# Second MLP matmul as seven block products, in a two-layer decoder trunk on eight cores

## The chip, the cores and the metric

One Trainium2 chip, all 8 cores. Each core runs the same program on its own two of the 16 sequences (4096 tokens); the cores do not exchange data. The metric is the device time of one execution in microseconds, that of the slowest core. TensorE does the matmuls, VectorE, ScalarE and GpSimd the elementwise work, and each of these engines works through its own queue strictly in order.

## The reference

Two layers on h of shape (16, 2048, 1024), D_MODEL 1024, D_FF 4096, and a final norm:

```python
def squared_relu_mlp(h, w1, w2):
    a = jax.nn.relu(h @ w1)
    return (a * a) @ w2

for i in range(DEPTH):               # DEPTH = 2
    if i == 0: h = h + conv_mixers(rms_norm(h, ...), ...)
    else:      h = h + chunked_spatial_gating(rms_norm(h, ...), ...)
    h = h + squared_relu_mlp(rms_norm(h, mlp_norm_g[i]), mlp_w1[i], mlp_w2[i])
return rms_norm(h, final_norm_g)
```

Only the MLP is changed. Its two matmuls are 1024 x 4096 and 4096 x 1024 for each token.

## The kernel before

A core makes four passes (`mt`) over 1024 tokens each. In a pass: mixer 0, MLP 0, mixer 1, MLP 1. `h` (float32) and the transposed normed activations `xnT` (float16) stay in SBUF for the pass. There are 8 PSUM banks, handed out from a list in order of release (`get_bank`, `put_bank`).

**Weights** are cut into pieces, which go through 7 slots of 8 KB per partition in a fixed order; `release(i)` frees a slot and at once asks for the next pieces. On its first use a piece is *fresh*: it is read as float32 and cast by the DMA, which GpSimd's queue issues; the prepared piece is then written to a cache in DRAM (`wcache`). Later passes load it from there, issued by the SP queue. Which pass is the first use for the cache is `first_mt`: for `w1_1` passes 0 and 1 both load fresh and pass 1 stores.

**The MLP** (`mlp`) runs in four quarters `fq` of the hidden width, each first matmul, then second.

First matmul: four pieces a quarter. `Job` computes 128 x 2 hidden columns for all 1024 tokens as a 2 x 2 block product with seven products instead of eight (Winograd's form). One product is 4 matmuls of 128 x 128 on 128 x 512. The operands on the activation side are four blocks of `xnT` and four sums of them (`Xs`, made by `xsum`); on the weight side four blocks and four differences, made on VectorE by `prep` for fresh pieces (for a cached piece they come with it). The methods are A (products m1, m2), B7 (m7), B6 (m6), C (m5), D4 (m4), D3 (m3). m6, m5 and m3 accumulate into the bank of m1, and m4 into that of m7; between them ScalarE takes a copy (`snap`) and VectorE adds the bank to such a copy (`via`). So each of these products must wait until the reader before it has read the bank. Then comes `relu_sq`: relu on ScalarE, square on GpSimd into `hid` (bf16). A block's last three steps (C, D4, D3) run interleaved with the next block's first ones. The first two pieces of quarter 0 are computed plainly (`plain_part`, `PLAIN = 2`), while `xsum` runs.

Second matmul: two pieces of 1024 x 512 (bf16) a quarter; 8 token blocks x 2 halves, 8 matmuls each, and VectorE adds each bank to `h` (`add_to_h`). The first ones (`early`) are put between D4, C and D3 of the last block. In quarters 0 to 2 `prep_to` prepares the next quarter's first-matmul pieces meanwhile.

In layer 1 of passes 0 to 2, `pre_step` puts the loads, statistics (`stat_tb`, square with accumulation) and scaling (`xn_op`) of the next pass's x into quarters 0 to 2.

All queue orders are the order in which the program text calls the helpers; waits are derived from which tile regions and banks an operation reads and writes (`Prog.op`).

## Time and profile before

| | |
|---|---|
| time, median of 3 runs | 2651.98 us (2647.46 to 2652.52) |
| profiled execution, its time | 2627.72 us |
| its span, slowest core | 2625.2 us (all cores 2617.5 to 2625.2) |
| granted TensorE clock, mean | 0.993 of full on seven cores, 0.992 on one |
| instructions of TensorE | 12952 matmuls |
| busy: TensorE, VectorE, ScalarE, GpSimd | 97%, 53%, 41%, 30% |
| DMA | 361.33 MB, mean 138 GB/s |

The profile is of one execution. Its rows name a line of the kernel, the engine, the operation, and the tiles written and read; Z is the big SBUF region that holds the weight slots, `hid`, `Xs` and the buffers. L926 is the second MLP matmul, L838 the seven-product first matmul, L909 the plain part, L438 a helper for all two-input elementwise operations (`tt`), L823 relu, L845 `snap`, L787 `add_to_h`. PE is TensorE, PEld its weight load, DVE VectorE, ACT ScalarE, POOL GpSimd.

### The profile page before, as it was taken

The page shows a single profiled execution, that of the slowest core. Times are in us where ns is not written, and L with a number is a line of the kernel's source. Part 1 is how long each engine was busy: PE and PEld are TensorE (multiplying, and loading weights), DVE is VectorE, ACT ScalarE, POOL GpSimd, SP SyncE. Part 2 cuts the span into 40 slices and gives each one's busy share as a digit, 9 for nine tenths or more (in the row PEclk, how much of TensorE's full clock was granted, in tenths as well). Part 3 has the DMA queues.
Part 4 walks back from the last instruction along what each step waited for, and adds up shares of the span by engine and source line. Part 5 has one row for each costly group of instructions (what it writes and reads, how often), then busy time and mean ns, then how long its engine had stood idle before and what let it go on. Part 6 is the DMA issues. An engine that isn't in the chain of part 4 may idle for free.

```text
span 2625.2 us, 40635 instructions; the slowest of 8 cores (2617.5 to 2625.2 us)
## 1 busy us (share of the span) xinstructions
PE 2546.0 (97%) x12952; PEld 1217.5 (46%) x12952; DVE 1386.0 (53%) x2269; ACT 1070.2 (41%) x1808; POOL 792.3 (30%) x1012
## 2 busy tenths in 40 slices
PE   5879999999999999999999999999999999999998
PEld 2534444444454444444455444454445444445443
DVE  4755446654566334664457533564345753357334
ACT  2433245434344226534524423643443433364323
POOL 2025342533303223333410323233430034314323
PEclk9989999999999999999999999999999999999999
DMA  9868894676763223167565223214446333312322
GB/s 192 210 145 201 193 200 121 130 146 137 240 193 106 105 91 119 41 176 197 163 198 189 89 105 121 72 53 165 149 145 213 113 119 117 127 36 100 119 89 81
DMA packets 121904, 361.33 MB, mean 138 GB/s; under 512 B 24416, under 2 KB 70496, under 8 KB 104672
## 3 DMA queue, kind: packets, MB, share of 16 engines
q1 hardware_dynamic: 73536, 230.67, 25.6%
q0 software_dynamic: 37072, 55.58, 14.0%
q10 hardware_dynamic: 11088, 72.49, 7.8%
q8 instruction: 108, 1.77, 0.3%
q14 instruction: 100, 0.82, 0.1%
HBM read 326.20 MB, written 88.08 MB: 158 GB/s over the span
## 4 chain that ended last, share of the span: by engine, by line
PE 87%; DMA 6%; DVE 4%; issue 2%; ACT 1%; SPq 0%; ACTq 0%; DVEq 0%; POOL 0%; POOLq 0%
PE bank L926 34%; PE bank L838 25%; PE bank L779 11%; PE bank L766 10%; DMA scr_s<-Z 3%; DVE Z L438 2%; PE bank L605 2%; PE bank L909 2%; PE bank L1049 1%; DMA scr_a<-Z 1%; DMA Z<-scr_s 1%; PE bank L715 1%; PE bank L1288 1%; DMA h<-x 0%; DMA Z<-scr_a 0%
## 5 line engine op out<-in xcount | busy, mean ns | idle before, releaser
L926 PE MATMUL bank<-Z 128*128 128x512 bf16 x4096 | 910.3, 379 | 0.0
L438 POOL TENSOR_TENSOR Z<-Z 128x512 bf16<-128x512 f32 x512 | 530.4, 1049 | 740.7 <-PE bank L838 370.1
L787 DVE TENSOR_TENSOR h<-bank,h 128x512 f32<-128x512 f32 x640 | 430.9, 688 | 477.2 <-PE bank L926 384.8
L926 PEld LDWEIGHTS bank<-Z 128*128 128x128 bf16 x4096 | 399.5, 98 | 475.4
L438 DVE TENSOR_TENSOR Z<-bank,Z 128x512 f32<-128x512 f32 x336 | 232.2, 692 | 482.4 <-PE bank L838 466.6
L838 PE MATMUL bank<-Z 128*128 128x512 f16 x1792 | 430.1, 380 | 10.8 <-DVE Z L438 10.7
L845 ACT ACTIVATE Z<-bank 128x512 f32<-128x512 f32 x336 | 190.2, 589 | 530.1 <-PE bank L838 527.7
L766 PE MATMUL bank<-xnT,Z 128*128 128x512 f16 x1792 | 399.2, 382 | 3.0 <-DVE xnT L617 3.0
L823 ACT ACTIVATE Z<-Z 128x512 f32<-128x512 f32 x336 | 211.4, 629 | 331.7 <-DVE Z L438 331.6
L838 PE MATMUL bank<-xnT,Z 128*128 128x512 f16 x1344 | 327.0, 379 | 0.0
L838 PEld LDWEIGHTS bank<-Z 128*128 128x128 f16 x1792 | 174.9, 98 | 225.0 <-issue 16.2
L766 PEld LDWEIGHTS bank<-xnT,Z 128*128 128x128 f16 x1792 | 175.5, 98 | 212.7 <-issue 11.1
L558 ACT ACTIVATE junk<-h 128x1024 bf16<-128x1024 f32 x136 | 143.6, 1056 | 279.1 <-DVE h L787 265.4
L838 PEld LDWEIGHTS bank<-xnT,Z 128*128 128x128 f16 x1344 | 131.6, 98 | 158.9 <-issue 1.0
L625 POOL TENSOR_SCALAR st<-st 128x1 f32<-128x1 f32 x160 | 36.7, 229 | 504.2 <-ACT junk L558 502.8
L779 PE MATMUL bank<-Z 128*128 128x512 bf16 x832 | 186.1, 379 | 0.0
L617 DVE TENSOR_TENSOR xnT<-bank,sm 128x1024 f16<-128x1024 f16 x96 | 116.2, 1219 | 46.0 <-PE bank L605 46.0
L823 ACT ACTIVATE Z<-bank 128x512 f32<-128x512 f32 x176 | 102.6, 588 | 85.1 <-PE bank L909 57.9
L779 PEld LDWEIGHTS bank<-Z 128*128 128x128 bf16 x832 | 79.8, 98 | 89.8
L909 PE MATMUL bank<-xnT,Z 128*128 128x512 f16 x512 | 115.7, 379 | 0.0
L779 PE MATMUL bank<-Z,xnT 128*128 128x512 f16 x512 | 115.1, 379 | 0.0
L573 ACT ACTIVATE xn_tm<-h,st 128x1024 f16<-128x1024 f32 x100 | 113.6, 1136 | 3.0 <-POOL st L438 2.5
(99 smaller groups left out, 1726.2 us busy)
## 6 DMA issues: line engine op xcount, KB each, us to landing
Z<-wcache SPq DMA_DIRECT2D x66, 1024.0 KB, 5.0
Z<-wcache SPq DMA_DIRECT2D x55, 896.0 KB, 4.6
wcache<-Z ACTq DMA_DIRECT2D x29, 1024.0 KB, 8.6
wcache<-Z SPq DMA_DIRECT2D x28, 896.0 KB, 7.9
Z<-w POOLq DMA_DIRECT2D x48, 512.0 KB, 6.4
Z<-wcache ACTq DMA_DIRECT2D x21, 1024.0 KB, 6.5
h<-x SPq DMA_DIRECT2D x32, 512.0 KB, 10.0
Z<-w POOLq DMA_DIRECT2D x16, 1024.0 KB, 12.9
```

Of the source, the lines that this page charges most:

```text
L438: P.op(eng, lambda e: e.tensor_tensor(out=out, in0=in0, in1=in1, op=op), reads=reads, writes=writes)
L558: small("act", lambda e: e.activation(out=junk[:], in_=ap, func=AF.Square, scale=1.0 / 32, accum_out=st[:, c0 + tb:c0 + tb + 1]), keys, [( ...
L573: small("act", lambda e: e.activation(out=out, in_=ap, func=AF.Copy, scale=col), keys + [("st", c0 + 8 + tb)], okeys)
L617: small("dve", lambda e: e.tensor_tensor(out=xnT[:, :, tb * 128:(tb + 1) * 128], in0=tbk.rearrange("p (k n) -> p k n", k=8), in1=gcol.unsq ...
L766: r = e.matmul(banks[b][:], lhsT=where[slot].v[:, kc, m * 128:(m + 1) * 128], rhs=xnT[:, kc, s * 512:(s + 1) * 512], start=(kc == 0), stop ...
L779: r = e.matmul(banks[b][:], lhsT=lhs(kc, tb), rhs=where[slot].v[:, kc, :], start=(kc == 0), stop=(kc == 7))
L787: small("dve", lambda e: e.tensor_tensor(out=h[:, tb, d * 512:(d + 1) * 512], in0=banks[b][:], in1=h[:, tb, d * 512:(d + 1) * 512], op=ALU ...
L823: small("act", lambda e: e.activation(out=t_.v, in_=src, func=AF.Relu), rkeys, t_.k())
L838: ins = e.matmul(banks[bank][:], lhsT=t_.v[:, wb, kc * 128:(kc + 1) * 128], rhs=xf(kc), start=start and kc == 0, stop=stop and kc == 3, sk ...
L845: small("act", lambda e: e.activation(out=t_.v, in_=banks[b][:], func=AF.Copy), [("ps", b)], t_.k())
L909: r = e.matmul(banks[b][:], lhsT=t_.v[:, kc // 4 * 2 + k, kc % 4 * 128:kc % 4 * 128 + 128], rhs=xnT[:, kc, s_ * 512:(s_ + 1) * 512], start ...
L926: r = e.matmul(banks[b][:], lhsT=lhs(kc, tb), rhs=where[slot].v[:, kc, :], start=start and x_ == 0, stop=stop and x_ == len(ks) - 1)
```

## The change

- In quarters 0 to 2 the second matmul too is computed with seven block products. The hidden activations are stored in float16 in `hid`, and their sums s1, s2, s4 in `Hs` (s3 takes the place of block a21, in `hid` and in `xnT`). `hsum` makes the sums of a hidden column group in four VectorE steps. `W2Job` is one of four 128-token blocks: seven products of 4 matmuls. Its results are scaled by 256 and reach `h` by a VectorE step and an addition on GpSimd (`via`), the last one by VectorE alone.
- The second matmul's weights of these quarters are four pieces instead of two, prepared by `prep` and cached like the first matmul's (3.5 KB of columns instead of 4). Their `first_mt` in layer 1 is 1. A pass has 73 pieces instead of 61. Quarter 3 keeps the plain form (`w2z`), in float16.
- `prep` has three VectorE steps, one of them of double size, instead of four.
- The square runs on ScalarE; of the four blocks of a first-matmul piece, the one of D4 gets relu and square together in one VectorE step after the addition. The relu scales by 1/16.
- The order around the turn from the first to the second matmul is new, and the second matmul's first blocks are interleaved with the last W1 block; from then on blocks overlap across the quarter boundary.
- `rbuf` has 7 buffers instead of 10.

```diff
 def first_mt(i):
-    return 1 if pieces[i][0] == "w1_1" and n_mt > 1 else 0
+    return 1 if pieces[i][0] in ("w1_1", "w2_1") and n_mt > 1 else 0
...
 def prep(i):
-            for d, a_, b_ in ((4, 1, 0), (5, 3, 4), (1, 3, 1), (6, 2, 5)):
+            P.op("dve", lambda e: e.tensor_tensor(out=v[:, 0:3:2, :], in0=v[:, 2:5:2, :], in1=v[:, 1:3, :], op=ALU.subtract),
+                 reads=t_.ki(1, 3) + bk(4), writes=bk(0) + bk(2))
+            for d, a_, b_ in ((5, 4, 0), (6, 3, 5)):
                 tt("dve", v[:, d, :], v[:, a_, :], v[:, b_, :], ALU.subtract, bk(a_) + bk(b_), bk(d))
...
+        SUM_A = (("s1", "a21", "a22", ALU.add), ("s3", "a11", "a21", ALU.subtract))
+        SUM_B = (("s2", "s1", "a11", ALU.subtract), ("s4", "a12", "s2", ALU.subtract))
...
         def relu_sq(src, rkeys, t_, row, col):
-            small("act", lambda e: e.activation(out=t_.v, in_=src, func=AF.Relu), rkeys, t_.k())
-            tt("pool", hid.v[:, col, row * 512:(row + 1) * 512], t_.v, t_.v, ALU.mult, t_.k(),
-               hid.k(col * T + row * 512, col * T + (row + 1) * 512))
+            small("act", lambda e: e.activation(out=t_.v, in_=src, func=AF.Relu, scale=RSC), rkeys, t_.k())
+            small("act", lambda e: e.activation(out=hid.v[:, col, row * 512:(row + 1) * 512], in_=t_.v, func=AF.Square),
+                  t_.k(), hid.k(col * T + row * 512, col * T + (row + 1) * 512))
...
+        class W1Job(Job):
+            def via(self, b0, t_, row, k):
+                if (row, k) != (0, 0):
+                    tt("dve", t_.v, banks[b0][:], t_.v, ALU.add, [("ps", b0)] + t_.k(), t_.k())
+                    relu_sq(t_.v, t_.k(), t_, row, 4 * k + self.m)
+                    return
+                P.op("dve", lambda e: e.scalar_tensor_tensor(out=t_.v, in0=banks[b0][:], scalar=RSC, in1=t_.v,
+                                                             op0=ALU.mult, op1=ALU.add), [("ps", b0)] + t_.k(), t_.k())
+                P.op("dve", lambda e: e.scalar_tensor_tensor(out=hid.v[:, self.m, 0:512], in0=t_.v, scalar=0.0, in1=t_.v,
+                                                             op0=ALU.max, op1=ALU.mult), t_.k(), hid.k(self.m * T, self.m * T + 512))
...
+        class W2Job(Job):
+            wscale = rscale = HSC
+            def via(self, b0, t_, row, d):
+                P.op("dve", lambda e: e.scalar_tensor_tensor(out=t_.v, in0=banks[b0][:], scalar=HSC, in1=t_.v,
+                                                             op0=ALU.mult, op1=ALU.add), [("ps", b0)] + t_.k(), t_.k())
+                tb = 4 * row + self.cp
+                hv, hk = h[:, tb, d * 512:(d + 1) * 512], [("h", tb, d)]
+                tt("pool", hv, hv, t_.v, ALU.add, hk + t_.k(), hk)
...
+            def run(job, prev, mid=None):
+                job.A()
+                if prev is not None:
+                    prev.C()
+                if mid is not None:
+                    mid()
+                job.B7()
+                job.B6()
+                if prev is not None:
+                    prev.D4()
+                    prev.D3()
...
+                p, l = prev, w1(fq, 3)
+                l.A()
+                p.C()
+                l.B7()
+                p.D4()
+                if strassen and not (fq == 0 and PLAIN == 2):
+                    sums(1)
+                p.D3()
+                l.B6()
+                if strassen:
+                    ii = [take((f"w2_{L}", fq, m))[0] for m in range(4)]
+                    prep_to(OFF[fq] + 8)
+                    w = [W2Job(ii, c) for c in range(4)]
+                    w[0].M1()
+                    l.D4()
+                    w[1].M1()
+                    sums(2)
+                    l.C()
+                    w[0].M2((0, 1, 2))
+                    l.D3()
+                    sums(3)
+                    w[1].M2((0, 1, 2))
+                    w[0].B7((0, 1, 2))
+                    w[1].B7((0, 1, 2))
+                    w[2].M1()
+                    w[0].M2((3,))
+                    w[1].M2((3,))
+                    w[0].B7((3,))
+                    w[1].B7((3,))
+                    prep_to(OFF[fq] + 9)
+                    w[0].B6()
+                    w[1].B6()
+                    w[0].C()
+                    w[0].D4()
+                    w[2].M2()
+                    w[0].D3()
+                    w2_done(fq, 0)
+                    w[1].C()
+                    w[2].B7()
+                    w[1].D4()
+                    w[2].B6()
+                    w[1].D3()
+                    w2_done(fq, 1)
+                    prep_to(OFF[fq] + 10)
+                    run(w[3], w[2])
+                    w2_done(fq, 2)
+                    prep_to(OFF[fq] + 11)
+                    prev = w[3]
```

`M1` and `M2` are the two halves of A; `w1()` takes a piece and prepares up to it; `w2_done(fq, c)` calls `pre_step` for token blocks 2c and 2c + 1. `sums(m)` calls `hsum` for hidden column group m; its sums need all four blocks of that group. In quarter 0, `sums(0)` and `sums(1)` are made during the first block, in quarters 1 and 2 `sums(0)` in the third block and `sums(1)` as shown.

## Rows read from the trace of the kernel before

**Rows 1.** The page: busy shares, clock in 40 slices, chain that ended last.

```profile
PE 2546.0 (97%) x12952; PEld 1217.5 (46%) x12952; DVE 1386.0 (53%) x2269; ACT 1070.2 (41%) x1808; POOL 792.3 (30%) x1012
...
PEclk9989999999999999999999999999999999999999
...
PE 87%; DMA 6%; DVE 4%; issue 2%; ACT 1%; SPq 0%; ACTq 0%; DVEq 0%; POOL 0%; POOLq 0%
```

**Rows 2.** Windows, one quarter: busy PE, PEld, DVE, ACT, POOL; clock; DMA share; GB/s.

```profile
1548.14:1599.93 51.79, 51.79 (x241) 23.49 (x240) 19.09 (x28) 15.77 (x28) 16.37 (x17) 1.00 0.31 112
```

**Rows 3.** Critical chain in order of time, pass 2: start us, us, what.

```profile
1548.30 23.74 PE bank L926 x110
1572.04 21.58 PE bank L838 x100
```

**Rows 4.** Groups by line and form, whole span: busy us, mean ns, idle before.

```profile
L438 POOL TENSOR_TENSOR Z<-Z 128x512 bf16<-128x512 f32 x512 | 530.4, 1049 | 740.7 <-PE bank L838 370.1 <-ACT Z L823 365.0 <-DVE Z L438 4.4
...
L438 DVE TENSOR_TENSOR Z<-bank,Z 128x512 f32<-128x512 f32 x336 | 232.2, 692 | 482.4 <-PE bank L838 466.6 <-ACT Z L845 8.0
L823 ACT ACTIVATE Z<-Z 128x512 f32<-128x512 f32 x336 | 211.4, 629 | 331.7 <-DVE Z L438 331.6
L845 ACT ACTIVATE Z<-bank 128x512 f32<-128x512 f32 x336 | 190.2, 589 | 530.1 <-PE bank L838 527.7 <-POOL Z L438 0.5 <-ACT Z L823 0.4
...
L1108 DVE TENSOR_TENSOR Z<-Z 128x1024 f32<-128x1024 f32 x32 | 39.0, 1220 | 1.7
...
L1171 DVE SCALAR_TENSOR_TENSOR Z<-Z,sm 128x512 f32<-128x512 f32 x32 | 24.1, 752 | 3.3
```

**Rows 5.** Timeline, turn to the second matmul: start, us, what, idle before.

```profile
1596.91 1.03 PE L838 MATMUL bank<-Z 128*128 128x512 f16 x4
...
1598.05 0.69 DVE L438 TENSOR_TENSOR Z<-bank,Z 128x512 f32<-128x512 f32 x1 [0.97 <-PE bank L838]
...
1599.07 1.03 PE L838 MATMUL bank<-Z 128*128 128x512 f16 x4
...
1600.31 0.60 ACT L823 ACTIVATE Z<-bank 128x512 f32<-128x512 f32 x1 [0.84 <-PE bank L838]
```

**Rows 6.** Timeline, first seven-product block of pass 0, then of quarter 1.

```profile
195.66 1.08 DVE L438 TENSOR_TENSOR Z<-xnT,Z 128x512 f16<-128x512 f16 x1
...
199.03 1.62 DVE L438 TENSOR_TENSOR Z<-Z 128x512 f16<-128x512 f16 x4
...
200.46 1.89 PE L838 MATMUL bank<-Z 128*128 128x512 f16 x8 [2.72 <-DVE Z L438]
...
291.40 0.69 DVE L530 TENSOR_TENSOR Z<-bank,sm 128x512 f32<-128x512 f32 x1 [0.20 <-PE bank L526]
...
292.27 0.69 DVE L534 TENSOR_TENSOR biasT<-Z 128x512 f32<-128x512 f32 x1 [0.17 <-DVE Z L530]
...
295.78 1.55 ACT L845 ACTIVATE Z<-bank 128x512 f32<-128x512 f32 x3
```

**Rows 7.** Window around the end of a pause; columns as in rows 2.

```profile
80.00:85.00 5.00, 3.33 (x16) 2.33 (x17) 1.22 (x2) 0.44 (x1) 0.00 (x0) 0.50 0.53 155
```

**Rows 8.** Timeline of TensorE, the same matmuls after a pause and without.

```profile
81.67 10.27 PE L1049 MATMUL bank<-Z 128*128 128x256 bf16 x72 [5.59 <-DVE Z L1070]
...
2010.11 8.05 PE L1049 MATMUL bank<-Z 128*128 128x256 bf16 x72
```

**Rows 9.** Waits of TensorE: us in total, times, longest.

```profile
PE bank L838 <- DVE Z L438: 10.7, 7, 2.7
```

**Rows 10.** Timeline of ScalarE, statistics and scaling of the next pass's x.

```profile
578.80 1.04 ACT L558 ACTIVATE junk<-Z 128x1024 bf16<-128x1024 f32 x1
...
579.84 1.13 ACT L573 ACTIVATE xn_tm<-Z,st 128x1024 f16<-128x1024 f32 x1
```

**Rows 11.** DMA, 40 slices of 1560 to 1605; issues in 318 to 370.

```profile
GB/s 0 0 0 0 0 0 0 0 0 0 80 306 393 401 433 148 0 0 0 0 217 382 217 0 0 89 325 395 6 0 205 376 242 0 0 0 66 357 408 124
...
Z<-w POOLq DMA_DIRECT2D x2, 1024.0 KB, 16.1
```

More of the change, by code:

```diff
@@ L183 @@
 PLAIN = 2
+RSC = 1.0 / 16
+HSC = 256.0
 WX_N = NG * NLAG * NPH
@@ L350, in blocks @@
         def blocks(i):
[L351 removed]
+            return pieces[i][0] in ("w1_0", "w1_1", "w2_0", "w2_1")
         def plain(i):
[L354 removed]
+            return pieces[i][0][:2] == "w1" and pieces[i][1] == 0 and pieces[i][2] < PLAIN
         def first_mt(i):
[L357 removed]
+            return 1 if pieces[i][0] in ("w1_1", "w2_1") and n_mt > 1 else 0
         def fresh(i):
@@ L369, in place @@
             wn, r0, _ = pieces[i]
-            last = wn == "w2_1" and r0 == 3072
+            last = wn == "w2z_1"
             top = LOW if low_only[0] or wn.startswith("ev") or last else NSLOT
-            order = list(range(LOW, top)) + list(range(LOW)) if blocks(i) else list(range(top))
+            order = list(range(top))
             order = [q for q in order if q not in live.values()]
@@ L375, in place @@
                 return None
-            if not blocks(i):
-                order = [q for q in order if q < LOW] or order
+            want = [q for q in order if (q < LOW) == (wn[:2] != "w1")]
+            order = want or order
             q = min(order, key=lambda q: freed[q])
@@ new lines, in mm, with go @@
+            def mm(self, nm, bank, start, stop, ks=(0, 1, 2, 3)):
+                fn, keys = self.operands(nm, ks)
+                def go(e):
+                    for x_, kc in enumerate(ks):
+                        l, r = fn(kc)
+                        ins = e.matmul(banks[bank][:], lhsT=l, rhs=r, start=start and x_ == 0,
+                                       stop=stop and x_ == len(ks) - 1, skip_group_check=True)
+                    return ins
+                P.op("pe", go, reads=keys, writes=[("ps", bank)])
@@ L834, in mm @@
                 xf, keys = xop(a_)
-                def go(e):
-                    for kc in range(4):
-                        ins = e.matmul(banks[bank][:], lhsT=t_.v[:, wb, kc * 128:(kc + 1) * 128], rhs=xf(kc),
-                                       start=start and kc == 0, stop=stop and kc == 3, skip_group_check=True)
-                    return ins
-                P.op("pe", go, reads=keys + t_.ki(wb), writes=[("ps", bank)])
-            def snap(self, b):
-                t_ = rb()
-                small("act", lambda e: e.activation(out=t_.v, in_=banks[b][:], func=AF.Copy), [("ps", b)], t_.k())
-                return t_
@@ L932, in part, with w1 @@
                     used(slot)
+            OFF = [0, 8, 16, 24]
+            def run(job, prev, mid=None):
[9 more added lines that the diff above has]
+                    prev.D3()
+            def w1(fq, m):
+                i = take((f"w1_{L}", fq, m))[0]
+                prep_to(i - base + 1)
+                return W1Job(i, m)
@@ L959, in mlp @@
+                p2 = [take((f"w2z_{L}", 0, d * 512))[0] for d in range(2)]
+                post, flush = tail
                 head, rest = (0, 1, 4, 5, 2, 6), (3, 7)
```

217 lines of the change are left out of this document (134 added, 83 removed).

## Prediction, made before the kernel was run

> **What bounds the kernel now.** I read the page first. Its busy shares [rows 1] give TensorE 97% of the span, every other engine about half or less, and a granted clock at the upper level of 2.4 GHz but for three of the first four slices. The chain of work that ended last [rows 1] runs for 87% on TensorE. I then cut an MLP stage into its quarters: the windows of three in a row read alike, and one of them [rows 2] shows TensorE busy for the whole 51.79 us, at full clock, with VectorE at 19.1, ScalarE at 15.8 and GpSimd at 16.4 us. So inside the MLP only two things set the time: how many matmuls there are, and every moment at which TensorE has to wait. The critical chain in order of time [rows 3] gives the price of one matmul: 23.74 us / 110 = 21.58 us / 100 = 0.2158 us.
>
> **Removed: matmuls.** A quarter of the second matmul is 128 matmuls, 8 token blocks x 2 halves x 8. As seven products it is 4 blocks x 7 x 4 = 112. Three quarters in each of 8 MLPs (4 passes x 2 layers) drop 16 each: 384 x 0.2158 = **82.9 us less**. The format moves nothing: of the two pieces of chain in [rows 3] the first is bf16, the second float16, at one price. GpSimd loses all 512 squares; ScalarE and VectorE gain the work, and neither is full on average (ScalarE about 29 us per new quarter of 48: 24 snapshots at 0.589 and 24 relu or square steps at 0.63 [rows 4]). Averages do not decide it; the order in the queues does.
>
> **Added: the turn from the first matmul to the second.** Take T = 0 where the first product of the second matmul starts, with no stall. TensorE's queue is then: w0.M1, l.D4 (0.86 to 1.73 us), w1.M1, l.C (2.59 to 3.45), three matmuls of w0.M2, l.D3 (wants to start at 4.10). l.D3 accumulates into the bank that l.C's addition on VectorE must have read. VectorE's queue in front of that addition, in order: the two steps of l.D4, four float16 sums (`sums(2)`), then the addition. The timeline [rows 5] shows a VectorE step beginning 1.14 us after the first of its four matmuls (1596.91 to 1598.05). The D4 pair: 0.69, the start of a dependent step 0.18 behind it (291.40 + 0.69 to 292.27 [rows 6]), second step 0.70 (between the f32 two-input row, 0.692, and the nearest SCALAR_TENSOR_TENSOR row, 0.752 [rows 4]). Four chained float16 steps take 1.62 us [rows 6], the addition 0.69, and TensorE resumes 0.2 later (third of the four preparations ends at about 200.26, TensorE at 200.46 [rows 6]). So 0.86 + 1.14 + 0.69 + 0.18 + 0.70 + 1.62 + 0.69 + 0.2 = 6.1 against 4.10: **2.0 us of waiting**, bounds 1.8 and 2.3. Before, six matmuls and one addition stood there, and no time was lost [rows 5]. In the 15 quarters whose pieces come prepared from the cache: 15 x 2.0 = +30.
>
> **The same turn with fresh weights.** The pieces of w2_0 in pass 0 and of w2_1 in passes 0 and 1 are fresh (w2_1's cache is now filled in the second pass): 9 quarters. There `prep_to(OFF+8)` puts the preparation of all four pieces, 12 VectorE steps, into the queue ahead of l.D4. Two steps of each are the known ones (1.62/4 = 0.405). The third has 1024 elements: not in the trace in float16, at least 0.405, at most the 1.22 of the f32 row [rows 4]; I take 0.67, the known step plus the 0.27 that 512 more elements cost at the slope of the f16 step (0.405 less a fixed part of about 0.14, which the f32 step, 0.69 at twice the slope, leaves). A piece: 1.48; four: 5.9 (4.9 to 8.1). In quarters 1 and 2, VectorE gets to them late: p.D4's product starts at T-2.59, its pair on VectorE at T-1.45, which ends at T+0.1, and sums(1) at T+1.8. Then 1.8 + 5.9 + 1.6 + 1.65 + 0.69 + 0.2 = 11.8 against 4.10: 7.7 us, 6 times: +46 (6.6 to 9.8 each). In quarter 0 sums(1) is done earlier and the chain starts at T-0.4: 5.5, 3 times: +17 (4.4 to 7.6 each).
>
> A page would make this cheaper. The Trainium skill, VectorE: DVE Perf Modes (section "The TRN2 errata"), gives 58 + elements/2 cycles for such a float16 step, 0.33 us; no row here is so short, [rows 6] has 0.405 from start to start. By it a piece would cost 1.25 and my whole sum would be about 8 us lower; the row decides.
>
> **The clock.** In a pause of 5.59 us TensorE's granted clock fell to 0.50, the 1.2 GHz level [rows 7], and the 72 matmuls behind it took 10.27 us where the same 72 later took 8.05 [rows 8]. After a pause of 2.72 us eight took 1.89, the full rate [rows 6]. So each of the nine long stalls costs 0 to 2.2 us more; they are as long as the longer pause, so I take 2.2: +20. The 2.0 us stalls cost none.
>
> The Trainium skill, TensorE: Matmul & The Clock Gate (section "Loop structure matters more than you think"), marks a VectorE copy between matmul groups as something that does not break the warm clock, and only a long DMA wait as what does. Read so, this term is 0 and my sum 20 lower; but the 5.59 us pause in [rows 8] was itself a wait for VectorE.
>
> **Smaller terms.**
> - w0.C follows w0.B6 by one product (0.86 us) but needs its snapshot: ScalarE starts 1.24 after the first of four matmuls, 0.38 after their end [rows 5]; 0.59, 0.1 to resume. 0.15 to 0.2 x 24 = +4.
> - In passes 0 to 2 of layer 1, quarters 1 and 2, two statistics and two scalings (1.04 and 1.13 [rows 10], some 4.2 together as their starts overlap the ends before) now stand on ScalarE in front of w3's first snapshot, behind one scaling that waits for GpSimd's three h additions. Counted from the end of w1.B6: GpSimd gives the scaling its value at 6.1, that and w2's snapshots end at 8.2, the four steps at 12.4, w3's snapshot at 13.0; w3.B6 wants the bank at 11.2. With 0.1 to resume, 6 x 1.9 = +11 (0 to 18).
> - Fresh quarter 0: preparing the last w1 piece pushes p.C's addition past p.D3: 3 x 1.4 = +4.
> - Preparing the next w1 pieces beside GpSimd's additions: a float16 step beside a busy GpSimd lasts 1.08 us instead of 0.405 [rows 6]. Three such before w0.C's addition delay w0.D3 by about 1: +9 (0 to 27).
> - The same effect, undone: the plain part no longer squares on GpSimd, so its 16 sums end sooner and the 10.7 us that TensorE now waits there [rows 9] goes: -10.
> - GpSimd's h additions, 12 x 1.05 us per 48 us quarter, are behind nothing that TensorE needs: cover is the gap to the next use of the buffer, over 4 us.
> - DMA, cached: the pieces of a quarter are asked for 18 us (three of w2 and one of w1) and 12 us (the last) before T. A pair of pieces moved at 306 to 433 GB/s in four slices of 1.1 us [rows 11]; five of 896 KB at 400 are 11.5 us: hidden. Fresh: two pieces of 1024 KB written, with twice that read, took 16.1 us [rows 11]; five half-size pieces about 20 against 18. Late by 2, this hides behind VectorE's own lateness above; more than 4 late it would not.
>
> **Sum.** -83 + 30 + 46 + 17 + 20 + 4 + 11 + 4 + 9 - 10 = **+48 us** on the profiled execution's 2627.7 (span 2625.2, 2.5 around it): 2676. That execution was 0.9% below the median of the runs, 2651.98; in the same ratio, **2700**. With every term at its lower bound the sum is about -14 (2638), with all at the upper about +110 (2763): the likeliest case's own range.
>
> **Rivals.**
> - *The likeliest, 0.66*: as summed, 2700.
> - *Fresh preparation stays off the path, so the change is faster, 0.17.* If VectorE gets the 12 steps done before l.D4, the nine fresh turns cost 2 us each like the others: -83 + 30 + 18 + 4 + 11 + 4 + 9 - 10 = -17, 2635 on the median's scale. For it: VectorE has 32 us free in a quarter [rows 2] and the pieces can land before T. Against: the queue is in order and these steps stand where they stand. It decides when a fresh turn, clock included, costs under 3.9 us rather than 9.2. A fuller form, in which l.D3's wait is gone too, ends near 2586.
> - *Weights late, 0.12.* Fresh pieces land 5 us later than VectorE needs them, since store-backs grow from 4 x 896 + 2 x 1024 to 8 x 896 KB a quarter and move at the same time: 9 x 5 more, 2745. Against: raw bytes loaded per quarter do not grow.
> - *ScalarE becomes the limit of the first matmul, 0.05.* Nine steps per block at 0.5 us by their starts (three in 1.55 [rows 6]) plus dependencies are 5.3 of 6.04 us. If it were 6.5, 112 blocks x 0.46 = +52: 2752.
>
> **How the numbers follow.** A measurement tells about 0.2% (5 us) from no change. The likeliest case lies above +5 in nine parts of ten; the two slow rivals do wholly; the fast one hardly. Slower: 0.60 + 0.17 = 0.77, same 0.07, faster 0.16. The range 2632 to 2752 leaves out the fuller fast form and the worst of the slow ones.
>
> **What would show it.** After: 12568 matmul instructions; TensorE waiting for VectorE at the product line 24 times, 15 near 2 us and 9 of 5 to 8 us with a granted clock of 0.5 behind them; waits for ScalarE of about 2 us six times; plain parts without a wait. I am wrong if the fresh turns wait under 4 us, or if the long waits name a DMA.

## The result, and the profile after

**Slower, by 2.43%.** The ratio of the changed kernel's runs to those of the kernel before is 1.0243, 95% interval 1.0161 to 1.0325, from runs of 2702.66, 2713.20 and 2728.96 us. (In some executions of either kernel one or both dies ran at a lower granted clock, in two of the changed kernel's three timed runs too, whose median of 2886.3 us says nothing of the change; such runs are left out here, and "core median" below is the median span over the cores of those dies whose four cores all have a mean granted clock of 0.96 or more.) The forecast was 2700, slower, for nearly the reasons given, and on the scale of the profiled execution it was too low: 2676 against 2702.66. That execution's slowest core, 7, has a span of 2701.1 us, where the kernel before had 2625.2: 75.9 us to account for.

The page of the changed kernel, busy shares, clock, the chain that ended last, and the group of the second matmul's additions on GpSimd:

```profile
PE 2527.5 (94%) x12568; PEld 1186.5 (44%) x12568; DVE 1654.8 (61%) x2831; ACT 1404.1 (52%) x2384; POOL 637.7 (24%) x812
...
PEclk9899999998999999998999999999999999999999
...
PE 79%; DVE 10%; issue 4%; DMA 4%; ACT 2%; POOL 1%; DVEq 0%; ACTq 0%; SPq 0%; POOLq 0%
...
L446 POOL TENSOR_TENSOR h<-h,Z 128x512 f32<-128x512 f32 x288 | 365.9, 1289 | 667.7 <-DVE Z L965 667.5
```

The 384 matmuls are gone as counted (12568 left), yet TensorE's busy time fell by only 18.5 us instead of 83, mostly because its mean clock fell (54 us of the terms below); and VectorE's part of the chain went from 4% to 10% [rows 1]. Where TensorE now waits, from the view of its waits (us in total, times, longest); L871 is the seven-product matmul, L446 the two-input elementwise helper, L879 the snapshot, L1016 the plain second matmul of quarter 3, L965 the second matmul's scaled addition, L455 the 1024-wide preparation step:

```profile
PE bank L871 <- DVE Z L446: 76.7, 27, 8.0
PE bank L871 <- ACT Z L879: 16.6, 8, 2.8
...
PE bank L871 <- DMA Z<-w: 10.8, 4, 4.1
...
PE bank L1016 <- DMA Z<-w2z: 6.0, 2, 4.8
PE bank L871 <- DVE Z L965: 3.9, 9, 0.7
...
PE bank L871 <- DVE Z L455: 1.8, 3, 0.6
```

The waits at this product line were 10.7 us before [rows 9]. The cores of one execution differ in how these waits are named: on the eight cores of this one the first row is 70.0 to 88.1 us and the one for fresh weights, `Z<-w`, 1.4 to 20.3, but their sum is 87.4 to 92.5 on each; where the weights land late, VectorE catches up meanwhile. So the two are compared below as a sum. The wait for `w2z` ranges from nothing to 15.8 us.

**A cached quarter.** The same window as [rows 2], from one turn to the next; first core 0 of the changed kernel, then core 4 of the same execution:

```profile
1630.85:1681.25 50.40, 48.64 (x224) 21.78 (x225) 27.98 (x48) 27.31 (x49) 15.01 (x12) 1.00 0.39 146
...
1625.89:1677.42 51.53, 49.76 (x225) 22.07 (x226) 28.11 (x48) 27.46 (x49) 15.02 (x12) 0.98 0.38 143
```

On core 0 it takes 50.40 us: 224 x 0.2158 = 48.34, the wait of 1.77, and 0.3 that a pause costs beyond what its row says. Of that, 0.17 is how the last matmuls are drawn (four take 1.03 us in their row, and the next four start 0.86 after them); the rest no row explains. The saving is 51.79 - 50.40 = 1.39 us of the 3.45 that 16 matmuls are worth. Core 4 shows something else: the same work at a granted clock of 0.98, 1.13 us longer. More on that below.

**A fresh turn.** VectorE's timeline in pass 0 of layer 1, and TensorE's beside it:

```profile
600.77 1.81 DVE L446 TENSOR_TENSOR Z<-Z 128x512 f16<-128x512 f16 x4
602.50 0.69 DVE L455 TENSOR_TENSOR Z<-Z 128x1024 f16<-128x1024 f16 x1
603.30 0.95 DVE L446 TENSOR_TENSOR Z<-Z 128x512 f16<-128x512 f16 x2
...
609.15 0.68 DVE L942 SCALAR_TENSOR_TENSOR Z<-bank,Z 128x512 f32<-128x512 f32 x1
609.94 0.69 DVE L944 SCALAR_TENSOR_TENSOR Z<-Z 128x512 f16<-128x512 f32 x1
610.55 1.81 DVE L446 TENSOR_TENSOR Z<-Z 128x512 f16<-128x512 f16 x4
612.28 0.68 DVE L446 TENSOR_TENSOR Z<-bank,Z 128x512 f32<-128x512 f32 x1
```

```profile
601.69 1.03 PE L871 MATMUL bank<-xnT,Z 128*128 128x512 f16 x4
602.55 2.54 PE L871 MATMUL bank<-Z 128*128 128x512 f16 x11
613.11 1.44 PE L871 MATMUL bank<-Z 128*128 128x512 f16 x3 [8.02 <-DVE Z L446]
```

The row at 601.69 is l.D4 (its operand a22 lies in `xnT`), so T, where w0.M1 starts, is 600.83. The queue is the one of the forecast, step for step: sums(1), until T + 1.7; four preparations of 1.66 each, until T + 8.3; the D4 pair; sums(2); l.C's addition; and 0.15 later TensorE, at T + 12.3. l.D3 could have started at T + 4.1, eleven matmuls of 0.2158 behind 602.55. The granted clock behind it, in windows of 1 and 2 us:

```profile
613.00:614.00 1.00, 0.89 (x3) 0.37 (x4) 0.00 (x0) 0.85 (x2) 0.00 (x0) 0.50 0.00 0
...
617.00:618.00 1.00, 1.00 (x4) 0.34 (x3) 0.00 (x0) 0.00 (x0) 0.00 (x0) 0.50 0.40 57
618.00:620.00 2.00, 2.00 (x10) 0.86 (x9) 0.19 (x1) 0.42 (x1) 0.00 (x0) 0.92 1.01 201
```

Some 5 us at the 1.2 GHz level after a pause of 8.02 us: about 2.6 us lost.

### The profile page after: what moved, and what is told of

Same layout as the page of the kernel before. It is cut to its first block, busy times and chain, and to the rows that moved or that the text cites. A ratio compares the mean times of both kernels' runs of the same rounds, so it can differ in the third digit from the quotient of the medians.

```text
span 2701.1 us, 41222 instructions; the slowest of 8 cores (2681.0 to 2701.1 us)
## 1 busy us (share of the span) xinstructions
PE 2527.5 (94%) x12568; PEld 1186.5 (44%) x12568; DVE 1654.8 (61%) x2831; ACT 1404.1 (52%) x2384; POOL 637.7 (24%) x812
## 4 chain that ended last, share of the span: by engine, by line
PE 79%; DVE 10%; issue 4%; DMA 4%; ACT 2%; POOL 1%; DVEq 0%; ACTq 0%; SPq 0%; POOLq 0%
PE bank L871 40%; PE bank L789 11%; PE bank L776 9%; PE bank L1016 8%; PE bank L999 4%; DVE Z L446 4%; PE bank L1207 2%; PE bank L615 2%; PE bank L725 2%; DVE Z L455 1%; DMA Z<-w2z 1%; DMA scr_s<-Z 1%; DVE Z L942 1%; DVE Z L944 1%; DVE Z L1329 1%
## 5 line engine op out<-in xcount | busy, mean ns | idle before, releaser
L871 PE MATMUL bank<-Z 128*128 128x512 f16 x4032 | 966.0, 389 | 108.7 <-DVE Z L446 76.7
L871 PEld LDWEIGHTS bank<-Z 128*128 128x128 f16 x4032 | 396.8, 100 | 629.7 <-issue 211.1
L879 ACT ACTIVATE Z<-bank 128x512 f32<-128x512 f32 x624 | 353.4, 590 | 343.4 <-PE bank L871 335.0
L446 POOL TENSOR_TENSOR h<-h,Z 128x512 f32<-128x512 f32 x288 | 365.9, 1289 | 667.7 <-DVE Z L965 667.5
L871 PE MATMUL bank<-xnT,Z 128*128 128x512 f16 x1792 | 450.2, 389 | 1.9 <-DVE Z L455 1.8
L965 DVE SCALAR_TENSOR_TENSOR Z<-bank,Z 128x512 f32<-128x512 f32 x288 | 193.8, 689 | 217.9 <-PE bank L871 194.5
L446 DVE TENSOR_TENSOR Z<-Z 128x512 f16<-128x512 f16 x540 | 232.0, 446 | 79.4 <-ACT Z L859 42.8
L871 PEld LDWEIGHTS bank<-xnT,Z 128*128 128x128 f16 x1792 | 178.4, 100 | 225.5 <-issue 45.2
L859 ACT ACTIVATE Z<-Z 128x512 f16<-128x512 f32 x400 | 252.2, 631 | 39.3 <-ACT Z L858 2.2
L1016 PE MATMUL bank<-Z 128*128 128x512 f16 x1024 | 233.7, 381 | 6.0 <-DMA Z<-w2z 6.0
L446 DVE TENSOR_TENSOR Z<-bank,Z 128x512 f32<-128x512 f32 x224 | 151.9, 689 | 121.6 <-PE bank L871 66.8
L798 DVE SCALAR_TENSOR_TENSOR h<-bank,h 128x512 f32<-128x512 f32 x224 | 152.6, 689 | 109.3 <-PE bank L1016 71.8
L789 PE MATMUL bank<-Z 128*128 128x512 bf16 x832 | 186.1, 379 | 0.0
L942 DVE SCALAR_TENSOR_TENSOR Z<-bank,Z 128x512 f32<-128x512 f32 x112 | 77.4, 691 | 142.7 <-PE bank L871 131.3
L1016 PEld LDWEIGHTS bank<-Z 128*128 128x128 f16 x1024 | 99.0, 98 | 120.4 <-issue 8.6
L803 DVE TENSOR_TENSOR h<-bank,h 128x512 f32<-128x512 f32 x128 | 86.0, 687 | 85.3 <-PE bank L789 60.5
```

The costliest lines, as they stand in the source:

```text
L446: P.op(eng, lambda e: e.tensor_tensor(out=out, in0=in0, in1=in1, op=op), reads=reads, writes=writes)
L789: r = e.matmul(banks[b][:], lhsT=lhs(kc, tb), rhs=where[slot].v[:, kc, :], start=(kc == 0), stop=(kc == 7))
L798: small("dve", lambda e: e.scalar_tensor_tensor(out=h[:, tb, d * 512:(d + 1) * 512], in0=banks[b][:], scalar=scale, in1=h[:, tb, d * 512:( ...
L859: small("act", lambda e: e.activation(out=hid.v[:, col, row * 512:(row + 1) * 512], in_=t_.v, func=AF.Square), t_.k(), hid.k(col * T + row ...
L871: ins = e.matmul(banks[bank][:], lhsT=l, rhs=r, start=start and x_ == 0, stop=stop and x_ == len(ks) - 1, skip_group_check=True)
L879: small("act", lambda e: e.activation(out=t_.v, in_=banks[b][:], func=AF.Copy, scale=sc), [("ps", b)], t_.k())
```

## The experiments

Core medians of the kernel before on the three chips used: 2621.9, 2624.1 and 2622.6 us. The changed kernel, run once more (the last experiment), has 2688.9, and the differences below are taken from that. In its first measurement it had 2699.5; there all eight cores of the profiled execution lost 9 to 33 us to stretches at a granted clock of 0.81, which the last experiment takes up. Rows of waits are those of the slowest core, and line numbers are shifted by one or two in some of the edited kernels (L872 and L873 are the product line L871). Experiment 4 edits the kernel before, where it is L838.

**1. sums(2) behind l.C's addition**

```diff
-                    sums(2)
                     l.C()
+                    sums(2)
                     w[0].M2((0, 1, 2))
```

> The changed kernel with one swap: sums(2) stands behind l.C instead of in front of it in VectorE's queue. Theory (the wait at l.D3 is VectorE's queue: the D4 pair, four sums, then the addition that l.D3 needs): without the 1.8 us of sums in front, the fifteen waits of 1.77 to 2.21 us fall to about 0.3 to 0.5, and the nine fresh ones by up to 1.8 us each: 24 x 1.4, about 34 us less than the changed kernel (2702 to about 2668). Rival (the wait only moves, since w0.B7 needs the sums of group 2 that now come later): as many us of waits in all, time within 5 us of 2702. Rival on the clock (the stretches at a granted 0.81 follow from the pauses): they go with the pauses and the time falls by 10 to 25 us more.

Measured: core median 2641.6, 47 us below the changed kernel, where I expected 34. The slowest core took 2710.31 us, but in that execution cores 2 and 3 show long stretches at a granted clock of 0.81 (on core 3 from 390 to 554 us, for one), so the core median says more. These stretches are there although the waits are gone, which speaks against the rival that they follow from the pauses. Its waits, and a cached quarter on core 0:

```profile
PE bank L871 <- DVE Z L446: 29.9, 27, 5.9
PE bank L871 <- DMA Z<-w: 21.4, 6, 7.0
```

```profile
1610.24:1659.18 48.94, 48.64 (x226) 21.79 (x225) 27.98 (x48) 27.31 (x49) 15.01 (x12) 1.00 0.41 152
```

The cached turns wait 0.30 instead of 1.77 to 1.92 and the quarter takes 48.94 us, 2.85 less than before the change: the seven-product form pays, once VectorE's queue has the addition first. The waits for VectorE and for fresh weights together are 51.1 to 55.7 us on the eight cores, against 87.4 to 92.5: some 37 us less. The rest of the 47 fits the clock: the half-rate stretches cost core 0 25.7 us here, and 37 to 42 us in the changed kernel (experiment 10).

**2. The fresh w2 pieces prepared on GpSimd**

```diff
-            P.op("dve", lambda e: e.tensor_tensor(out=v[:, 0:3:2, :], in0=v[:, 2:5:2, :], in1=v[:, 1:3, :], op=ALU.subtract),
+            eng = "pool" if pieces[i][0][:2] == "w2" else "dve"
+            P.op(eng, lambda e: e.tensor_tensor(out=v[:, 0:3:2, :], in0=v[:, 2:5:2, :], in1=v[:, 1:3, :], op=ALU.subtract),
...
-                tt("dve", v[:, d, :], v[:, a_, :], v[:, b_, :], ALU.subtract, bk(a_) + bk(b_), bk(d))
+                tt(eng, v[:, d, :], v[:, a_, :], v[:, b_, :], ALU.subtract, bk(a_) + bk(b_), bk(d))
```

> The changed kernel with the preparation of w2 pieces on GpSimd instead of VectorE (27 steps of 512 and 1024 elements in nine quarters become GpSimd's). Theory (the fresh turns wait 3.3 to 8.0 us because twelve preparation steps stand ahead of l.D4 in VectorE's queue): those waits at the product line fall to those of the cached turns, 2 us, plus what float16 sums lose beside a busy GpSimd (0.7 us a step, up to 3 us per turn), or a wait for GpSimd of up to 4 us takes their place because four pieces cost it about 17 us; sum between -30 and +10 us against the changed kernel. Rival (weights that land late): the waits stay at 5 to 8 us or name a DMA.

Measured: ratio 1.0399 (1.0248 to 1.0551), core median 2719.1: 30 us worse than the changed kernel, outside the range that I expected. (The steps moved are 108, twelve in each of nine quarters, not 27.) The groups of float16 steps by form in this kernel, then the one of the changed kernel:

```profile
L446 DVE TENSOR_TENSOR Z<-Z 128x512 f16<-128x512 f16 x468 | 290.0, 638 | 69.0 <-ACT Z L860 38.2 <-DVE Z L456 2.4 <-DVE Z L446 1.4
L446 POOL TENSOR_TENSOR Z<-Z 128x512 f16<-128x512 f16 x72 | 86.6, 1203 | 10.3
L456 POOL TENSOR_TENSOR Z<-Z 128x1024 f16<-128x1024 f16 x36 | 80.0, 2222 | 0.1
```

```profile
L446 DVE TENSOR_TENSOR Z<-Z 128x512 f16<-128x512 f16 x540 | 232.0, 446 | 79.4 <-ACT Z L859 42.8 <-DVE Z L446 1.3 <-DVE Z L455 0.9
```

A piece takes GpSimd 4.6 us instead of VectorE's 1.66, and VectorE's own sums go from 446 to 638 ns beside it. Taking the 12 steps off VectorE did not shorten the fresh turns (waits 103.2 us instead of 76.7). In one of them the four sums of `sums(1)` stand on VectorE while GpSimd prepares the pieces from 618.88 on; alone they took 1.81 us in the turn above:

```profile
618.45 5.45 DVE L446 TENSOR_TENSOR Z<-Z 128x512 f16<-128x512 f16 x4
```

So this run leaves the queue of the forecast in place of the rival, late weights: the long waits still name VectorE, up to 10.5 us, and `Z<-w` has 12.6 us in four.

**3. The second pair of statistics behind w3's first snapshot**

```diff
-                    w2_done(fq, 1)
+                    if pre_mt:
+                        pre_step(pre_mt, fq, 2)
                     prep_to(OFF[fq] + 10)
-                    run(w[3], w[2])
+                    run(w[3], w[2], (lambda: pre_step(pre_mt, fq, 3)) if pre_mt else None)
```

> The changed kernel with the second half of a pre_step pair (one statistic and one scaling) moved behind w3's first snapshot. Theory (the six waits for ScalarE of 2.4 to 2.8 us at the product line come from four ScalarE steps of about 1.05 us in front of that snapshot): two steps less in front are 2.1 us less, so six waits of at most 0.7 us, about 13 us less. Rival (the wait moves to the next snapshots, s7 and s2 of w3): time unchanged within 5 us.

Measured: ratio 1.0267 (1.0177 to 1.0357), core median 2673.0, 16 us below the changed kernel. TensorE's waits for the snapshot fell from 16.6 us in 8 to 4.7 in 11, none above 0.7. So the six waits of 2.4 to 2.8 us were this queue. The other 4 us fit the half-rate stretches that stood behind four of the six.

**4. The kernel before, with its squares on ScalarE**

```diff
-            tt("pool", hid.v[:, col, row * 512:(row + 1) * 512], t_.v, t_.v, ALU.mult, t_.k(),
-               hid.k(col * T + row * 512, col * T + (row + 1) * 512))
+            small("act", lambda e: e.activation(out=hid.v[:, col, row * 512:(row + 1) * 512], in_=t_.v, func=AF.Square),
+                  t_.k(), hid.k(col * T + row * 512, col * T + (row + 1) * 512))
```

> The kernel before, with the 512 squares on ScalarE instead of GpSimd and nothing else. Theory on the queues: TensorE waits for nobody more; the 10.7 us that it waited in the plain parts go, since float16 sums no longer run beside GpSimd: 5 to 11 us faster than before. Rival on the clock: if ScalarE's load beside a full TensorE and full DMA is what brings the granted 0.81, such stretches show in this kernel too, 0 to 25 us slower than before.

Measured: ratio 1.0223 (1.0107 to 1.0340), core median 2669.5: 48 us slower than before. Both the theory (5 to 11 us faster) and the rival on the clock fail.

```profile
PE bank L838 <- DVE Z L438: 37.8, 24, 1.6
...
PE bank L838 <- ACT Z L845: 6.1, 30, 0.4
```

In the old order the nine ScalarE steps a block make VectorE's additions late: they wait 458.3 us in all for ScalarE's snapshots, where it was 8.0 before [rows 4]. TensorE then waits 1.57 us in each of 24 quarters, and with its own waits for snapshots 44 us in all; the granted clock stays at 0.991 to 0.994 on the cores. The changed kernel avoids this with the VectorE pair for the D4 block and its new order; its waits stand elsewhere.

**5. The changed kernel with the squares back on GpSimd**

```diff
-            small("act", lambda e: e.activation(out=hid.v[:, col, row * 512:(row + 1) * 512], in_=t_.v, func=AF.Square),
-                  t_.k(), hid.k(col * T + row * 512, col * T + (row + 1) * 512))
+            tt("pool", hid.v[:, col, row * 512:(row + 1) * 512], t_.v, t_.v, ALU.mult, t_.k(),
+               hid.k(col * T + row * 512, col * T + (row + 1) * 512))
```

> The changed kernel with the squares of relu_sq back on GpSimd (352 more steps of about 1.05 us there, as many fewer on ScalarE). My theory: the turn gets longer, because the float16 sums(2) on VectorE run beside a busy GpSimd (1.08 instead of 0.405 us a step, so up to 2.7 us more a turn) and the squares that the sums wait for end 0.5 us later: 24 x 2 = 48 us slower than the changed kernel, about 2750, ratio 1.04. Rival (the squares on ScalarE are the cost, as the kernel before with its squares on ScalarE was 50 us slower): this one is 20 to 40 us faster than the changed kernel, ratio 1.01.

Measured: 2770.93 and 2773.82 us, core median 2765.1, 76 us worse than the changed kernel, half as much again as I expected (400 steps moved, not 352).

```profile
PE bank L871 <- DVE Z L446: 102.5, 36, 8.0
PE bank L871 <- DVE Z L455: 19.6, 11, 5.6
PE bank L871 <- ACT Z L879: 17.6, 9, 2.8
```

```profile
L446 DVE TENSOR_TENSOR Z<-Z 128x512 f16<-128x512 f16 x540 | 299.5, 570 | 91.1 <-POOL Z L446 54.3 <-DVE Z L455 0.9 <-DVE Z L446 0.5
```

Both of the last two edits cost: squares on ScalarE in the old order, squares on GpSimd in the new one. The rival, that putting the squares back on GpSimd wins time back, is out.

**6. Layer 1's w2 stored to the cache in pass 0**

```diff
-            return 1 if pieces[i][0] in ("w1_1", "w2_1") and n_mt > 1 else 0
+            return 1 if pieces[i][0] == "w1_1" and n_mt > 1 else 0
```

> The changed kernel with only the cache rule of the second matmul's layer 1 pieces put back (stored in pass 0, read from the cache from pass 1 on). Pass 1 then has cached turns of 1.8 us instead of fresh ones of 5.5 to 8 us with their half-rate stretches: 3 x 6 = 18 us less than the changed kernel, 2685, ratio 1.017. Rival: pass 0 of layer 1 now writes 8 instead of 4 pieces back a quarter while it loads as many, and its waits for weights grow by as much as pass 1 gains: no difference.

Measured: 2691.14 to 2695.13 us, core median 2681.9, 7 us below the changed kernel, where I expected 18. The waits for VectorE and for fresh weights together are 75.4 to 82.3 us on the eight cores, against 87.4 to 92.5. By stage, that sum in layer 1 is 8.2 to 10.7 us in pass 1, where the changed kernel has 18.4 to 23.6, so pass 1 gains some 12 us, as the theory says. In pass 0 it is 18.5 to 22.3, where the changed kernel has 20.5 to 22.3: nothing is given back there, and the rival fails. The waits for w2z, 11.7 us a core on average, lie between the 5.9 and the 13.9 of the changed kernel's two profiled executions. Why only 7 of the 18 us show in the core median stays open.

**7. Edits 1, 3 and 6 together**

> The changed kernel with three edits at once: sums(2) behind l.C, w2_1 stored to the cache in pass 0 already (three fresh quarters fewer), and the second pair of statistics and scalings behind w3's first snapshot. If the waits I named are separate terms, they add: 15 cached turns at 0.3 instead of 1.8 us (-23), three fresh turns gone (3 x 6.5 = -20), the six left without sums(2) in front (6 x 1.6 = -10), ScalarE waits 17 to 4 (-12), and fewer long pauses (-8 of clock): some 73 us below the changed kernel, so 2625 to 2635, ratio 0.99 to 1.00. Rival (weights late): TensorE waits for the DMA of the fresh pieces instead; then the waits named Z<-w grow beyond 15 us and the time stays above 2650.

Measured: 2635.97 and 2637.36 us against 2631.72 and 2640.06 of the kernel before beside it, core median 2618.6. The single edits gave 47, 16 and 7 us, together 70, and 2688.9 - 70 is 2618.9: the three act as separate terms. That the sum closes so well leans on the 2688.9, which enters three times; from the 2699.5 of the first measurement it would be 2597.5. The rival, late weights, fails: on cores 4 to 7 (granted clock 0.983 to 0.989) the wait for fresh weights is up to 20.8 us, but together with that for VectorE 42.5 to 44.9 on each, and the time is under 2650. With the three edits the change is worth nothing by the slowest core and 5.5 us by the core median.

**8. The fresh preparation in stages**

On top of the three: m1 and m2 use raw blocks of the weights only, m7 needs the result of the 1024-wide step (0), m6 and m4 those of the other two (1 and 2), and `prep` takes the steps to make as a second argument (that edit is not shown, and some lines are joined here). So:

```diff
-                    prep_to(OFF[fq] + 8)
+                    prep_to(OFF[fq] + 4)
+                    ready[0] = OFF[fq] + 8
...
                     l.C()
-                    sums(2)
+                    sums(2, SUM_A)
+                    for i_ in ii[0:3]: prep(i_, (0,))
                     w[0].M2((0, 1, 2))
                     l.D3()
-                    sums(3)
+                    sums(2, SUM_B); sums(3, SUM_A); prep(ii[3], (0,)); sums(3, SUM_B)
                     w[1].M2((0, 1, 2))
+                    w[2].M1()
                     w[0].B7((0, 1, 2))
                     w[1].B7((0, 1, 2))
-                    w[2].M1()
...
                     w[1].B7((3,))
+                    for i_ in ii: prep(i_, (1,))
+                    for i_ in ii: prep(i_, (2,))
```

> The three edits, and the preparation of fresh w2 pieces in stages: the 1024-wide steps (needed by the m7 product only) behind l.C's addition and the first two sums, the two 512-wide steps and the store-backs behind the m7 products; w2.M1 stands ahead of them on TensorE. If the position of these 12 steps in VectorE's queue was what cost 5 to 8 us in a fresh turn, the waits for VectorE there fall to 0.3 at l.D3 and 1 to 2 at the m7 product, none with a long half-rate stretch behind it: 6 x 4 to 6 = 25 to 35 us less than the three edits alone, near 2600, ratio 0.98 to 0.99. Rival (weights late): the waits are renamed to the DMA, since TensorE is then at the pieces earlier; less than 10 us gained. Cached quarters should not differ from the three edits alone by more than 0.5 us each.

Measured: 2627.88 to 2634.71 us, core median 2617.0: against the three edits alone 6 us by the medians of the slowest core, 2 by the core median. I had expected 25 to 35. TensorE's timeline in a fresh turn, then VectorE's:

```profile
217.53 0.59 PE L873 MATMUL bank<-Z 128*128 128x512 f16 x2 [0.45 <-DVE Z L456]
222.76 5.54 PE L873 MATMUL bank<-Z 128*128 128x512 f16 x19 [4.64 <-DVE Z L446]
```

```profile
211.70 0.68 DVE L446 TENSOR_TENSOR Z<-bank,Z 128x512 f32<-128x512 f32 x1
212.30 0.94 DVE L446 TENSOR_TENSOR Z<-Z 128x512 f16<-128x512 f16 x2
213.16 1.89 DVE L456 TENSOR_TENSOR Z<-Z 128x1024 f16<-128x1024 f16 x3
214.97 1.81 DVE L446 TENSOR_TENSOR Z<-Z 128x512 f16<-128x512 f16 x4
216.70 0.69 DVE L456 TENSOR_TENSOR Z<-Z 128x1024 f16<-128x1024 f16 x1
217.30 0.95 DVE L446 TENSOR_TENSOR Z<-Z 128x512 f16<-128x512 f16 x2
218.17 1.28 DVE L967 SCALAR_TENSOR_TENSOR Z<-bank,Z 128x512 f32<-128x512 f32 x2
219.37 4.59 DVE L446 TENSOR_TENSOR Z<-Z 128x512 f16<-128x512 f16 x8
```

The waits at l.D3 and at m7 are nearly gone (0.30 to 0.56 and 0.45), but six of 4.64 us stand at w0.B6, which needs the t2 steps. So the wait moved rather than fell: VectorE and fresh weights together are 42.7 to 49.1 us on the eight cores, no less than with the three edits alone. VectorE has no gap for 12 us: the position of the steps was one part of the cost, their number is the other.

**9. The staged kernel with TensorE's gap filled**

```diff
+                    for i_ in ii[0:2]: prep(i_, (1,))
                     w[0].M2((3,))
                     w[1].M2((3,))
+                    for i_ in ii[2:4]: prep(i_, (1,))
                     w[0].B7((3,))
                     w[1].B7((3,))
-                    for i_ in ii: prep(i_, (1,))
+                    w[2].M2()
+                    w[2].B7()
                     for i_ in ii: prep(i_, (2,))
                     prep_to(OFF[fq] + 9)
                     w[0].B6()
                     w[1].B6()
                     w[0].C()
                     w[0].D4()
-                    w[2].M2()
+                    w[1].C()
                     w[0].D3()
                     w2_done(fq, 0)
-                    w[1].C()
-                    w[2].B7()
                     w[1].D4()
```

> The staged kernel, with two of the four t2 steps ahead of the last two m2 additions on VectorE, and on TensorE w2.M2 and w2.B7 (8 matmuls, 1.7 us) put ahead of w0.B6, the product that waited 4.64 us for t2 in the six fresh turns. If VectorE is only late for that one product, the wait falls to 1.5 to 2.5 us and the half-rate stretch behind it goes: 6 x 2.5 + 6 x 1.8 = some 25 us less than the staged kernel, 2605 to 2610, ratio to the kernel before 0.990. Rival: VectorE has more to do in a fresh turn than TensorE (its steps follow each other without a gap for 12 us there); then the wait moves to w0.D4, which needs t4, stays near 4 us in sum, and the time is that of the staged kernel, 2630.

Measured: **ratio 0.9929 (0.9881 to 0.9978)**, seven runs from 2618.73 to 2633.85 us, core median 2609.2: faster than both kernels. Its waits, and on core 5 three of the 2.07 us waits at w0.B6:

```profile
PE bank L873 <- DVE Z L446: 21.5, 33, 2.1
...
PE bank L873 <- DMA Z<-w: 10.7, 5, 7.1
...
PE bank L1018 <- DMA Z<-w2z: 6.7, 2, 4.6
```

```profile
529.66 4.92 PE L873 MATMUL bank<-Z 128*128 128x512 f16 x20 [2.08 <-DVE Z L446]
...
585.90 11.34 PE L873 MATMUL bank<-Z 128*128 128x512 f16 x44 [2.07 <-DVE Z L446]
...
642.46 1.89 PE L873 MATMUL bank<-Z 128*128 128x512 f16 x8 [2.07 <-DVE Z L446]
```

The waits fell from 4.64 to 2.07 us as expected; the gain of 8 us in the core median, of which 1.5 lie between the two chips, and of 11 in the medians of the slowest core, is under the 25 expected. Part of it went into ScalarE's snapshots (10.6 us in 17 waits instead of 3.5 in 10), and a pause of 2.07 us is still followed by the half rate at times, in three of six on core 5: the 44 matmuls at 585.90 took 11.34 us, 1.7 more than at the upper clock, the 8 at 642.46 the full-rate 1.89.

**10. The changed kernel once more**

> The changed kernel itself once more, beside the one above on the same chip. If the stretches at a granted clock of 0.81 belong to the kernel, they return, on several cores and in the same stages, and cost 5 to 25 us a core; if they belong to that execution or chip, they are gone, the cores differ by less, and the time is 2690 to 2700. The half-rate stretches should return in either case: some 20 a core, 35 to 40 us lost.

Measured: 2698.87 us, and a core median of 2688.9. In its profile, taken of a longer execution of 2776.21 us, windows of 1 us over the whole span of core 0 and of core 4 show no stretch at 0.81, and (1 - clock) x TensorE's busy time, summed over the stretches at 0.50, is 42 and 37 us in 23 and 20 of them. Cores 1 and 5 show none of length either. Cores 2, 3, 6 and 7 do, two on each die: core 6 shows 0.81 for 160 us on end, across stages; first core 6, then core 0 in the same window:

```profile
400.00:550.00 150.00, 150.00 (x717) 69.49 (x715) 84.26 (x179) 72.87 (x122) 35.04 (x59) 0.81 0.58 125
...
400.00:550.00 150.00, 142.72 (x793) 69.48 (x792) 104.80 (x227) 84.46 (x145) 35.34 (x58) 0.98 0.61 129
```

Cores that run the same program differ in it, and so do executions: in the first profile all eight cores had such stretches, most of them 6 to 15 us long. The kernel before has lower clocks on a pair of cores too (0.970 on cores 4 and 5, 0.99 on the other six, in an execution of 2685.94 us). So the 0.81 stretches come with an execution and a core, and nothing here ties them to the kernel's order of work; what grants them no run here shows. The half-rate stretches come back on every core looked at.

## Why the prediction was right, and where it was off

The forecast's terms against core 7 of the profiled execution, where each wait counts 0.3 more than its row, as in the cached quarter (the short ones of the w1 preparations 0.16, as their rows show no more):

| term | forecast | measured |
|---|---|---|
| 384 matmuls | -83 | -83 |
| 15 cached turns | +30 | +32 (27.7 in 15 waits of 1.76 to 2.21, and 15 x 0.3) |
| 9 fresh turns | +46 + 17 | +63 (VectorE 48.0, weights 10.8, and 13 x 0.3) |
| fresh quarter 0, w1 preparations | +4 + 9 | +9 (6.8 in 15 short waits) |
| snapshot of w0.C | +4 | under 1 |
| statistics in front of w3's snapshot | +11 | +18 (15.9 in six waits) |
| plain part | -10 | -13 |
| weights w2z of quarter 3 | none | +7 |
| half-rate stretches | +20 | +28 (36.4 us lost in 20 stretches; before 8.3 in 5), 13 of it in the fresh turns |
| granted clock of 0.81 | none | +26 on this core |
| waits in the mixers | none | -11 (8.5 of it the wait for `scr_s`, which is 7.9 to 13.1 on the cores of this one execution) |
| sum | +48 | +76 of 75.9 |

- **Matmuls, cached turns, fresh turns: right.** The position of l.C's addition behind the D4 pair and sums(2), and of 12 preparation steps in front of them, sets TensorE's waits; experiment 1 took the first away and 47 us with it; experiments 8 and 9 moved the second and cut it down. The nine fresh turns vary more than said. In quarter 0 they wait 5.59 to 5.95 us for VectorE, where 5.5 was forecast; in quarters 1 and 2 twice 8.02, where the weights were in time, and 6.14, 4.21, 3.29 and 0.90 behind waits of 1.90, 1.96, 2.89 and 4.06 for the DMA. The forecast named fresh turns under 4 us, or long waits that name a DMA, as signs of being wrong: two of the nine waits for VectorE are under 4, and one wait for the DMA is over it. With the wait in front of it counted, every fresh turn lies between 4.96 and 8.04, so the queue still sets the time, but the forecast took the weights as hidden and in four of nine turns they were not. A preparation took 1.66 us, not 1.48. The row decided rightly against the 1.25 that follows from the table of the Trainium skill, VectorE: DVE Perf Modes (section "The TRN2 errata"). The same section warns that this table's row comes out too low and gives a fixed part of about 150 cycles instead of 58; an estimate by that is 0.42 us for 512 elements and 0.69 for 1024, and the trace agrees with both (446 ns on average, and 0.69 at 602.50).
- **The clock term was mis-sized: 28, not 20.** I charged the nine fresh turns alone, 2.2 us each. Seven of them were followed by the half rate, 1.3 to 2.7 us each, some 13 us in all. The other 15 came where I had counted nothing: behind four of the six waits of 2.4 to 2.8 us for ScalarE, behind waits for weights and behind one cached turn, free to me by one row with 2.72 us in front of full rate [rows 6]. The waits for VectorE did break the clock, and moving the queue gave it back (experiment 9's cores have 0.987 to 0.992, the changed kernel's 0.976 to 0.979 in the 2698.87 us of experiment 10). So the reading by which this term was 0 fails. The section of TensorE: Matmul & The Clock Gate in the Trainium skill that it came from ("Loop structure matters more than you think") does not carry it either: in its sketch the next matmuls follow the copy at once, and here they waited up to 8.02 us for VectorE.
- **Statistics: mis-sized, 18 for 11.** GpSimd's additions to `h` take 1.29 us, not the 1.05 that I took from its squares, so that the scaling they gate is later: three of them make 0.7 of the 1 us that each wait is longer than forecast. Experiment 3 removed the waits.
- **Weights of quarter 3: missed.** I looked at the second matmul's new pieces only. All four pieces of a quarter stay in their slots until w3.D3, so w2z is asked for later than its equals were before; w, w2z and their store-backs share the DMA. These waits vary, from nothing to 16.7 us over the cores of the two profiled executions. The cause is read from the code and from the waits named w2z; no run here changed the slots alone.
- **0.81 stretches: not tied to the change.** Core 3, with a span of 2681.0 us, lost 11.8 us to them where core 7 lost 26; that is 14 of the 20 us between the two. By experiment 10 the kernel took 2698.87 us in an execution whose cores all have 0.976 or more. That the forecast of 2700 hits this is luck in part: its sum was too low by the clock and the statistics, and the 0.9% for the median, taken from other runs, made up for it. As a ratio to the kernel before, 1.018 was forecast and 1.0243 measured.
- **The rivals.** Fresh preparation off the path: no, it set the long turns. Weights late: a small part on core 7, 17 us with w2z, and mostly at the price of shorter waits for VectorE behind them. ScalarE as the limit of the first matmul: not in the new order; in the old one its squares cost 48 us.

## What to carry to other kernels

Fewer matmuls on a TensorE at 97% are worth their price only where the elementwise work that comes with them stays behind what TensorE waits for next: write down the order of the other engine's queue at the turn and put the step that frees a bank first. Here one swapped line was worth 47 us of the 66 lost, and the whole form, well ordered, ended at 0.9929. Work that is prepared for several products is best split by which product needs it, with TensorE's independent products put where the rest is late; and a long wait costs twice, once itself and once in the clock behind it.

## What the runs showed of the hardware that I had not expected

- Besides 0.50 and 1.00 the records show a granted clock of 0.81, for up to 160 us on end with TensorE busy throughout. In experiment 10 two cores of each die had it (2, 3, 6 and 7) and their neighbours on the same die did not.
- After pauses of 2.07 us TensorE came back at full rate in some cases and at the 1.2 GHz level for over 3 us in others (from about 586.2 to 589.6 on core 5 of experiment 9); after 8.02 us it took some 5 us to return.
- A float16 step of 512 elements on VectorE takes 446 ns on average in the changed kernel, 638 with the preparation on GpSimd, 570 with the squares there; beside a preparation on GpSimd four took 5.45 us, 1.36 each. GpSimd takes 1203 ns for the same step and 2222 for the 1024-wide one, VectorE 0.69 us for the latter in the fresh turn above.
- At the product line, waits for VectorE and for fresh weights trade against each other from core to core (70.0 to 88.1 and 1.4 to 20.3 us in one execution), while their sum is 87.4 to 92.5.
